# Expert down products all in fp32r, the weight rests made later, and three residual tiles parked in DRAM

## The reference, cut to what matters

```python
def swiglu(h, w_gu, w_down):
    gate, up = jnp.split(h @ w_gu, 2, axis=-1)
    return (jax.nn.silu(gate) * up) @ w_down

def moe_ffn(h, w_router, b_router, w_gu, w_down, w_sh_gu, w_sh_down):
    ...          # scores, top 8 experts of each of the 512 tokens, weights w
    def expert_block(acc, blk):
        tok, wts, e = blk
        out = swiglu(h_pad[tok], w_gu[e], w_down[e])
        return acc.at[tok].add(out * wts[:, None].astype(out.dtype)), None
    ...
    return acc[:N] + swiglu(h, w_sh_gu, w_sh_down)

x_lat = x_lat + gt2 * rms_norm(f_lat.reshape(B, T, D), g_post_ffn[l])
```

## Time and profile before

| | |
|---|---|
| three runs | 2118.14, 2121.33, 2124.74 us; median 2121.33 |
| the profiled execution | 2118.74 us, span of its trace 2117.0 us |
| PE busy | 2042.3 us (96% of the span) |
| DVE / ACT / POOL busy | 1311.6 / 1009.7 / 280.0 us |
| DMA, mean over the span | 186 GB/s; slices of the experts 235 to 385 GB/s |
| TensorE's granted clock | 0.991 of full speed, 1.00 in every stretch of the experts that is quoted below |

### The profile page before, as it was taken

One profiled execution on the slowest core, in us unless ns is written; L12 is line 12 of the kernel. 1 busy time (PEld: TensorE's weight loads), 2 busy tenths in 40 slices (PEclk: granted clock), 3 DMA queues, 4 the chain that ended last, 5 costly groups with the idle time before them and its releaser, 6 DMA issues.

```text
span 2117.0 us, 33346 instructions
## 1 busy us (share of the span) xinstructions
PE 2042.3 (96%) x12264; PEld 1695.0 (80%) x12265; DVE 1311.6 (62%) x1975; ACT 1009.7 (48%) x1475; POOL 280.0 (13%) x217
## 2 busy tenths in 40 slices
PE   8999989999999999999999998999999999999998
PEld 4888977889777667777777768998978898898898
DVE  4878587455788678888868866457642444423433
ACT  4345455223477567777767754334322224312322
POOL 0004032000122332233323310000000000000000
PEclk9999999999999999999999999999999999999999
DMA  9841111263799689999979972211122223222221
GB/s 358 268 145 61 59 45 68 89 253 131 287 346 362 235 302 358 359 361 368 374 264 385 349 278 97 80 61 61 59 81 82 98 83 107 100 80 100 100 80 61
DMA packets 77097, 393.56 MB, mean 186 GB/s; under 512 B 16369, under 2 KB 33009, under 8 KB 46481
## 3 DMA queue, kind: packets, MB, share of 16 engines
q1 hardware_dynamic: 57938, 358.38, 45.1%
q0 software_dynamic: 19008, 33.22, 6.3%
HBM read 384.56 MB, written 43.01 MB: 202 GB/s over the span
## 4 chain that ended last, share of the span: by engine, by line
PE 62%; DMA 5%; DVE 4%; ACT 2%; issue 2%; DVEq 0%; SPq 0%; POOLq 0%; ACTq 0%
PE bank L3449 17%; PE bank L2353 4%; PE bank L2379 4%; PE bank L2357 4%; PE bank L2356 4%; DMA moe_work<-in_experts_dram 3%; PE bank L3132 3%; PE bank L3134 3%; PE bank L3133 3%; PE bank L3117 2%; PE bank L3119 2%; PE bank L3118 2%; PE bank L2339 2%; DVE moe_gu_rest L2114 1%; PE bank L2382 1%
## 5 line engine op out<-in xcount | busy, mean ns | idle before, releaser
L2734 DVE TENSOR_TENSOR b_w_rest<-ring,b_w_high 128x2048 fp32r<-128x2048 f32 x63 | 144.4, 2292 | 180.2 <-ACT b_w_high L2729 179.8
L2353 PE MATMUL bank<-moe_gu_high,moe_x_high 128*128 128x512 f32 x512 | 209.7, 410 | 14.9 <-DVE moe_gu_rest L2114 8.0
L2729 ACT ACTIVATE b_w_high<-ring 128x2048 fp32r<-128x2048 f32 x63 | 120.5, 1913 | 178.4 <-PE bank L3449 126.7
L2357 PE MATMUL bank<-moe_gu_high,moe_x_rest 128*128 128x512 f32 x512 | 201.2, 393 | 0.0
L2356 PE MATMUL bank<-moe_gu_rest,moe_x_high 128*128 128x512 f32 x512 | 201.0, 393 | 0.0
L3133 PE MATMUL bank<-b_w_rest,b_h_high 128*128 128x256 f32 x608 | 171.7, 282 | 0.0
L3132 PE MATMUL bank<-b_w_high,b_h_high 128*128 128x256 f32 x544 | 156.8, 288 | 2.3 <-DVE b_h_rest L2764 1.1
L2114 DVE TENSOR_TENSOR moe_gu_rest<-moe_work,moe_gu_high 128x2048 fp32r<-128x2048 f32 x64 | 146.3, 2288 | 14.4 <-ACT moe_gu_high L1851 14.4
L3134 PE MATMUL bank<-b_w_high,b_h_rest 128*128 128x256 f32 x544 | 154.2, 284 | 0.0
L2114 DVE TENSOR_TENSOR moe_gu_rest<-ring,moe_gu_high 128x2048 fp32r<-128x2048 f32 x64 | 146.5, 2289 | 8.1 <-ACT moe_gu_high L1851 6.9
L3449 PE MATMUL bank<-b_w_high,hidden_high 128*128 128x256 f32 x512 | 144.9, 283 | 0.0
(11 more groups left out here) (525 smaller groups left out, 5340.7 us busy)
## 6 DMA issues: line engine op xcount, KB each, us to landing
ring<-in_stream_dram SPq DMA_DIRECT2D x101, 1024.0 KB, 4.9
moe_work<-in_experts_dram SPq DMA_DIRECT2D x32, 2048.0 KB
moe_work<-in_experts_dram SPq DMA_DIRECT2D x64, 1024.0 KB, 7.3
ring<-in_experts_dram SPq DMA_DIRECT2D x32, 2048.0 KB
X<-in_stream_dram SPq DMA_DIRECT2D x16, 512.0 KB, 9.3
mixer_work<-in_stream_dram SPq DMA_DIRECT2D x16, 512.0 KB, 8.8
mixer_work<-in_stream_dram SPq DMA_DIRECT2D x4, 1024.0 KB, 13.5
X<-in_x_dram SPq DMA_DIRECT2D x8, 512.0 KB, 10.6
```

The source lines that it names most:

```text
L2353: first = mm(banks[2][:, :], xh[:, k, :], wh[h][:, c], start=(k == 0), stop=False)
L2357: last = mm(banks[2][:, :], xl[:, k, :], wh[h][:, c], start=False, stop=(k == KD - 1))
L2734: nc.vector.tensor_tensor(WL[u % FEED], raw(u), high_at(u), ALU.subtract).then_inc(s["w_rest"], 1)
```

## The change

The down product becomes fp32r altogether. For each half k of the contraction there are now a high part DH[p][k] and a rest DL[p][k] of the down weight (two pieces of 128x1024 each on ACT and on DVE, where there was one), and one high part and one rest of the turned hidden rows, 128x256 wide (one piece each, where ACT had two of 128x128 and DVE one). PE issues 12 fp32r products for a block where it issued 2 plain ones (one for each half of the output, 4 records in all) and 6 fp32r ones. The rest of a down weight overwrites its slot.

On DVE dn_rest(u) stands behind w_rest(u+1, 1), and with it behind the further block, of which it stood ahead.

The new buffers lie in X's tiles 1, 2 and 3, so these three are stored to DRAM ahead of the experts (tiles 1 and 2 at the end of the mixer, among the stores of the normalised rows) and loaded back behind them: tile 1 where tile 3 was loaded, tile 3 behind unit 1 of the next block's weights, tile 2 once the last down product is done, ahead of units 2 and 3. Some scratch tiles of the further block move.

The diff, cut to its core (names of scratch tiles, waits that only change their counts in step, are left out):

```diff
@@ -477,8 +477,10 @@
             for t in range(NT):
                 sp.wait_ge(s["h2_ready"], t + 1)
                 sp.dma_start(dram["xn"][t * P:(t + 1) * P, :], H2[:, t, :]).then_inc(s["h2_stored"], 16)
+                if t in (1, 2):
+                    sp.dma_start(dram["parked"][t * P:(t + 1) * P, :], X[:, t, :]).then_inc(s["h2_stored"], 16)
             sp.wait_ge(s["zero_stored"], 32 * NT)
-            sp.wait_ge(s["h2_stored"], 16 * NT)
+            sp.wait_ge(s["h2_stored"], 16 * (NT + 2))
 
         @block.gpsimd
         def _(pool):
@@ -1545,13 +1547,14 @@
     ONEHOT = [grid(mem["place"](f"onehot{k}", EXACT + 816 + 256 * k, 512, BF16)[:, :], 4) for k in range(2)]
     ONEHOTX = grid(mem["place"]("onehot_further", EXACT + 1328, 512, BF16)[:, :], 4)
     CNT = take(NE).bitcast(I32)
-    SG, HID, HDT = take(256), take(256), [take(P) for _ in range(2)]
+    SG, HID = take(256), take(256)
     HDT_AT = at[0]
-    take(256)
-    HDTH = [exact(f"hidden_high{k}", AT_WORK + HDT_AT + P * k, P) for k in range(2)]
-    HDTL = [exact(f"hidden_rest{k}", AT_WORK + WORK + P * k, P) for k in range(2)]
-    DH = [exact(f"down_high{k}", o, D) for k, o in enumerate((AT_X + (NT - 1) * D, EXACT + 1712))]
-    DL = [exact(f"down_rest{k}", AT_WORK + 2 * GU + DN * k + D, D) for k in range(2)]
+    take(512)
+    HDTH = [exact(f"hidden_high{k}", AT_WORK + HDT_AT + 256 * k, 256) for k in range(2)]
+    HDTL = [exact(f"hidden_rest{k}", AT_ADAROW + 512 + 256 * k, 256) for k in range(2)]
+    DH_AT = ((AT_X + D, AT_X + 3 * D), (AT_X + 2 * D, EXACT + 1712))
+    DH = [[exact(f"down_high{p}{k}", DH_AT[p][k], D) for k in range(2)] for p in range(2)]
+    DL = [[exact(f"down_rest{p}{k}", AT_WORK + 2 * GU + DN * p + D * k, D) for k in range(2)] for p in range(2)]
 
     TOKI, ROWI = take(4).bitcast(I32), take(4).bitcast(I32)
     TWA, TWX = take(136).rearrange("p (e c) -> p e c", c=2), [take(2) for _ in range(2)]
@@ -1737,12 +1740,15 @@
             sums_back(1)
             sp.wait_ge(s["dn_done"], NE - 1)
             sp.wait_ge(s["rows_moved"], 32)
-            sp.dma_start(X[:, NT - 1, :], dram["last_rows"][:, :]).then_inc(s["rows_moved"], 16)
+            sp.wait_ge(s["shared_down_in"], 16)
+            sp.dma_start(X[:, 1, :], dram["parked"][P:2 * P, :]).then_inc(s["shared_down_in"], 16)
             unit_in(0)
             sums_back(2)
             sums_back(3)
             unit_in(1)
+            sp.dma_start(X[:, 3, :], dram["parked"][3 * P:4 * P, :]).then_inc(s["rows_moved"], 16)
             sp.wait_ge(s["dn_done"], NE)
+            sp.dma_start(X[:, 2, :], dram["parked"][2 * P:3 * P, :]).then_inc(s["rows_moved"], 16)
             unit_in(2)
             unit_in(3)
             then["sync"](sp)
@@ -1883,15 +1889,16 @@
             def copy_hdt(i, o):
                 after(act, "ht2_done", i, o, 1)
                 after(act, "dn_done", i, o - 2, 1)
-                nc.scalar.activation(HDTH[o % 2], banks[3][:, P:2 * P], ACT.Copy).then_inc(s["down_highs"], 1)
-                nc.scalar.activation(HDT[o % 2], banks[3][:, 0:P], ACT.Copy).then_inc(s["down_highs"], 1)
+                nc.scalar.activation(HDTH[o % 2], banks[3][:, 0:2 * P], ACT.Copy).then_inc(s["down_highs"], 1)
 
             def dn_high(i, o):
                 act.wait_ge(s_dn[o % 2], 16 * (o // 2 + 1) + 32 * i)
                 after(act, "dn_done", i, o - 2, 1)
                 if isinstance(i, int) and 4 * i + o == 0:
                     act.wait_ge(s["rows_moved"], 32)
-                nc.scalar.activation(DH[o % 2], dnslot[o % 2][:, D:2 * D], ACT.Copy).then_inc(s["down_highs"], 1)
+                for k in range(2):
+                    nc.scalar.activation(DH[o % 2][k], dnslot[o % 2][:, D * k:D * (k + 1)], ACT.Copy).then_inc(
+                        s["down_highs"], 1)
 
             def further_split(n):
                 for h in range(2):
@@ -2116,13 +2122,15 @@
 
             def dn_rest(i, o):
 
-                after(dve, "down_highs", i, o, 1, 3)
-                v.tensor_tensor(DL[o % 2], dnslot[o % 2][:, D:2 * D], DH[o % 2], ALU.subtract).then_inc(s["down_rests"], 1)
+                for k in range(2):
+                    after(dve, "down_highs", i, o, 1 + k, 3)
+                    v.tensor_tensor(DL[o % 2][k], dnslot[o % 2][:, D * k:D * (k + 1)], DH[o % 2][k], ALU.subtract).then_inc(
+                        s["down_rests"], 1)
 
             def hdt_rest(i, o):
 
                 after(dve, "down_highs", i, o, 3, 3)
-                v.tensor_tensor(HDTL[o % 2], banks[3][:, P:2 * P], HDTH[o % 2], ALU.subtract).then_inc(s["down_rests"], 1)
+                v.tensor_tensor(HDTL[o % 2], banks[3][:, 0:2 * P], HDTH[o % 2], ALU.subtract).then_inc(s["down_rests"], 1)
 
             def x_rest(i, o):
 
@@ -2169,10 +2177,10 @@
                     x_rest(i, u + 1)
                 if exists(i, u + 3):
                     indices(i, u + 3)
-                dn_rest(i, u)
-                more_blocks(dve, i, u, done, find_further, further)
                 if exists(i, u + 1):
                     w_rest(i, u + 1, 1)
+                more_blocks(dve, i, u, done, find_further, further)
+                dn_rest(i, u)
                 if exists(i, u + 2):
                     block_ahead(dve, i, u + 2, done, find_further)
                 if exists(i, u + 4):
@@ -2276,9 +2285,9 @@
             f_both(3)
             then["w_rest"](dve, 1)
             weighted(2)
+            dve.wait_ge(s["rows_moved"], 64)
             mixed(2)
             weighted(3)
-            dve.wait_ge(s["rows_moved"], 48)
             mixed(3)
             dve.wait_ge(s["f_tile"], 2 * NT)
             for t in (2, 3):
@@ -2360,29 +2369,26 @@
             def turn_hidden(i, o):
                 after(pe, "hid_ready", i, o, 1)
                 after(pe, "down_highs", i, o - 1, 3, 3)
-                after(pe, "down_rests", i, o - 1, 2, 2)
+                after(pe, "down_rests", i, o - 1, 3, 3)
                 for k in range(2):
                     last = nc.tensor.transpose(banks[3][:, k * P:(k + 1) * P], HID[:, k * P:(k + 1) * P], ident)
                 last.then_inc(s["ht2_done"], 1)
 
             def down_ready(i, o, bank=4):
                 after(pe, "down_highs", i, o, 3, 3)
-                after(pe, "down_rests", i, o, 2, 2)
+                after(pe, "down_rests", i, o, 3, 3)
                 if bank == 4:
                     after(pe, "out_act", i, o - 1, 2, 2)
-                pe.wait_ge(s_dn[o % 2], 16 * (o // 2 + 1) + 32 * i)
-
-            def down_products(bank, j, k, o, plain, high, rest):
-
-                c = slice(512 * j, 512 * (j + 1))
-                if k == 0:
-                    return mm(bank[:, :], plain, dnslot[o % 2][:, c], start=True, stop=False)
-                mm(bank[:, :], high, DH[o % 2][:, c], start=False, stop=False)
-                mm(bank[:, :], high, DL[o % 2][:, c], start=False, stop=False)
-                return mm(bank[:, :], rest, DH[o % 2][:, c], start=False, stop=True)
+
+            def down_products(bank, j, k, o, high, rest):
+
+                c, at = slice(512 * j, 512 * (j + 1)), slice(P * k, P * (k + 1))
+                mm(bank[:, :], high[:, at], DH[o % 2][k][:, c], start=(k == 0), stop=False)
+                mm(bank[:, :], high[:, at], DL[o % 2][k][:, c], start=False, stop=False)
+                return mm(bank[:, :], rest[:, at], DH[o % 2][k][:, c], start=False, stop=(k == 1))
 
             def down_part(i, o, j, k, bank=4):
-                product = down_products(banks[bank + j], j, k, o, HDT[o % 2], HDTH[o % 2], HDTL[o % 2])
+                product = down_products(banks[bank + j], j, k, o, HDTH[o % 2], HDTL[o % 2])
                 if (j, k) == (1, 1):
                     product.then_inc(s["dn_done"], 1)
 
@@ -2434,13 +2440,12 @@
                 last.then_inc(s["x_ht"], 1)
 
             def further_down(i, u, n):
-                pe.wait_ge(s["x_he"], 2 * n + 2)
+                pe.wait_ge(s["x_he"], n + 1)
                 pe.wait_ge(s["x_hid"], 2 * n + 2)
-                after(pe, "down_rests", i, u, 1, 2)
-                pe.wait_ge(s_dn[u % 2], 16 * (u // 2 + 1) + 32 * i)
+                after(pe, "down_rests", i, u, 2, 3)
                 for j in range(2):
                     for k in range(2):
-                        last = down_products(banks[6 + j], j, k, u, HDTX, HDTXH, HDTXL)
+                        last = down_products(banks[6 + j], j, k, u, HDTXH, HDTXL)
                     last.then_inc(s["x_dn"], 1)
                 pe.wait_ge(s["x_o"], 2 * n + 2)
 
```

20 lines of the change are left out of this document (10 added, 10 removed).

## The result

The changed kernel takes 2132.5 us (median of 4, 2131.03 to 2136.68); the kernel before, run beside it, 2121.1 us (2118.14 to 2124.74). The ratio is 1.0061, 95% interval 1.0049 to 1.0073: slower by 0.6%, where 0.4% faster (2113 us) was forecast, and outside the range of 2102 to 2127. The profiled execution took 2132.64 us (before: 2118.74), with a span of 2130.9 us.

What follows compares the result with a forecast made beforehand. PE was taken to bound the stage, transfers nearly full. Early experts -7.7, late ones -7.6, further blocks +7.4, start -1.2, end +0.6 summed to -8.5 us: 2121.3 became 2113 us, 8-in-10 range 2102 to 2127.

Steps and rivals of the forecast that it cites:

- Step 6: Further blocks: DVE's new order delays PE's products, +2.6 us a block less 0.2, +7.4 us for three; bounds +4 and +11.
- Step 1: PE's down product: 3.19 us becomes 2.87, saving 0.32 us an expert, so PE could go at 9.65 us.
- Step 2: DVE: a second down rest and a wider hidden rest make 9.75 us an expert; DVE becomes the bound at 9.77.
- DVE's waits stay: Rival, chance 0.13: DVE keeps waits behind PE for hidden(u) and x_rest; at half of them 10.45 us an expert, 2140 us.
- Step 3: ACT: one more high part brings its work from 7.63 to 8.6 us an expert, hidden under 9.77.
- Step 4: Order of rests: gate/up rest no longer behind a late down load, which may come about 2.5 us later before it costs.
- Step 5: Transfers: 376 GB/s taken for a long stretch, so a late expert takes 10.03 us; bounds 10.36 and 9.77.
- transfers at their limit: Rival, chance 0.25: 364 GB/s is all a long stretch gives, late experts stay at 10.36 us; 2126 us at worst.
- The limit of about 358 GB/s: HBM to SBUF transfers: a skill's limit for a core, by which nothing of PE's gain would come out; held for a rival.
- Step 7: Parking residual tiles in DRAM: nothing, at worst 2 us; the last expert's unhidden second down rest +0.6 us.
- only the late experts held by transfers: Case of the transfer rival: late experts gain nothing, early ones reach the forecast pace; 2123 us.
- w = 0.4: DVE's kept wait an expert from which it decides: 30 early experts gain 1.5 us in all, late ones 5, blocks take 7.4.

Runs made afterwards that it cites:

- e2: The kernel before with DVE's new order alone (gate/up rests, further block, then the one down rest), its products unchanged: 2124.2 us.
- e13: The changed kernel without the never-run code for a second and third further block, on PE, ACT and DVE: 2114.2 us.
- e17: The changed kernel with the never-run code for a second and third further block left out of PE's program alone: 2121.6 us.
- e18: The changed kernel with the never-run code for a second and third further block left out of DVE's program alone: 2125.7 us.
- e14: The changed kernel without the never-run code on PE, ACT and DVE, plus useless PE products in three waits of a further block: 2104.2 us.
- e5: The changed kernel with the second gate/up rests and both down rests moved inside the further block, behind its rows' rests: 2125.0 us.
- e10: The changed kernel with those rests inside the further block, but one DVE branch and one count load more per expert instead of two: 2126.6 us.
- e15: The changed kernel without the never-run code, with the rests inside the further block and one DVE branch more per expert: 2112.4 us.
- e1: The changed kernel with DVE's old order back (both down rests ahead of the further block and second gate/up rests): 2166.3 us.
- e8: The changed kernel without further blocks (rows beyond 128 left out), gathers and scatters cut to 16 rows: 2050.4 us.
- e12: The kernel before without further blocks (rows beyond 128 left out), gathers and scatters cut to 16 rows: 2065.6 us.
- e11: The kernel before with the parking alone (tiles 1 and 2 stored, three loads back with their waits): 2121.1 us against 2121.0.
- e9: The changed kernel with useless fp32r products given to PE ahead of three of its waits in a further block: 2273.1 us.

## Why the prediction was wrong

**Step 6, the further block, is the step that failed.** +7.4 us was the forecast, +11 its far end. The nine intervals 12 to 16 and 45 to 48 took 25.0 us more (4.0 + 11.9 + 9.2), though the ordinary ones among them should have gained 1 to 2. Two delays that the step named were there: 2.50 us of PE's idle time before the further down product, 7.5 in all, and DVE's gate/up rest ahead of the rows' rests. What its sum lacked is three terms:

- The search for the block, for which PE waited 5.4 us instead of 0.6. The step had it, a us for each, in its far end alone; the waits were 1.4, 1.6 and 2.4 us.
- A wait of 4.8 us for the gathered rows of the third block, which no step had. e2 has 7.4 us of such waits, e13, e17 and e18 have none, so it does not come every time, and what decides that is not settled.
- The clock. Behind some of these waits a few microseconds ran at half clock. By the rows that is at most (1 - 0.78) x 15.45 + 0.09 x 78.26 + 0.08 x 63.37 = 15.5 us, at most because it counts PE's idle time at half clock as lost too. e14 recovered 8.0 in two stages by keeping PE busy.

The windows of before for intervals 13 to 16 and 45 to 48 show how this adds up:

```profile
701.25:767.64 66.39, 61.96 (x286) 44.59 (x285) 38.86 (x61) 37.07 (x54) 18.89 (x11) 1.00 0.65 219
1051.80:1105.98 54.18, 51.18 (x242) 37.45 (x241) 36.87 (x57) 33.76 (x47) 17.77 (x10) 1.00 0.79 277
```

PE was idle for 4.4 + 3.0 us in them and is idle for 12.5 + 11.0 us in after: 16.1 of the 21.1 us more are waits. The other 5.0 are PE's busy time, which grew although its products take less: that is the clock.

The rests could also have stood in DVE's idle time of 5.78 us, which I read and set against nothing; there they take off 15 to 17 us (e5, e10).

**Step 1** was right: 2.86 us, products 0.23 us apart, intervals of 9.6 us.

**Step 2** mis-sized DVE. It is busy 151.89 / 16 = 9.49 us an expert, not 9.75, and hardly waits, so PE and DVE are nearly level at 9.5 to 9.6, and the rival "DVE's waits stay" is out. How little room DVE has shows when a branch is added (e10, e15: 0.3 us or more in three of four intervals).

**Step 3**: ACT is busy 132.72 / 16 = 8.3 us, hidden. Right.

**Step 4** was right and worth more than I gave it: with the old order the products cost 34 us more (e1). The chain of the earlier trace rows is gone, the wait of the earlier trace rows too.

**Step 5**, 376 GB/s in a long stretch: 371 in after, 383 in e18. Intervals 33 to 44 and 49 to 60 gained 6.7 us, near the 6.9 that 10.03 us an expert gives; that is luck in part, for the first twelve gained 0.8 and the last twelve 5.8. The rival "transfers at their limit" had the mechanism (e8, e12) but overstated it. The limit of about 358 GB/s that I weighed there does not bind here: 383 ran for 117 us. The Trainium skill (DMA: Bandwidth & Descriptors, section Bandwidth) gives it as the share of each core when both cores of a pair stream; with one core at work, as here, its own figure is the 425, and 383 is under that. So my sentence that by the page nothing would come out read it too narrowly.

**What no step had**: the first eleven intervals, +3.9 us (111.06 to 114.96) where 11 x 9.77 gives -3.6. e17 shows that it is PE's program: the three waits among the first eight experts. In the profile of before they were one wait of 1.2 us for nothing, at 619.77, which I let stand as one stall (2.6 us at the same place in e2, whose program on PE is the same). Why they grew to 7.1 us, when 9 packets came over q8 in both, is not settled; that a faster PE comes to its program sooner is a guess that no run tests.

**Step 7** was right: e11 is at 0.9984 to 1.0012, and the part behind the last load did not move.

Two sums among the rivals were wrong. With only the late experts held by transfers, -7.7 + 7.4 - 0.6 is -0.9, so 2120 us and not 2123. And at w = 0.4 the early experts take 10.15 us against 10.13, so they gain nothing, and not 1.5 us.

Of the 22 us between the sum of -8.5 and the 13.9 that came, the blocks with interval 12 explain some 19 and the first eleven intervals 7.5; the start, intervals 17 to 32 and 49 to 60 and the end were better than forecast and give the rest back.

## What to carry to other kernels

Where an engine waits in a rare block, count every wait, that of a search or gather ahead of the block too, and what PE's clock does behind it: here the blocks' two stages took 8.0 us less once PE was kept busy (e13, e14). Before rests or copies are moved behind a block, look for an idle stretch inside it. And count the code: the code of a branch that is never taken cost 18 us of 2132 here, and 192 more products in a loop's code some 150.

## What the hardware showed that was not expected

- PE's clock fell to half behind, or late in, 7 of the 12 waits of 1.4 us or more that PE had among the experts of after, and stayed full at the other five, among them two of 2.5 and 2.6 us. The same wait of 1.60 us ahead of the first further block was followed by half clock in after and by full clock in e13 and e17. Among the experts of before no wait was above 1.3 us, and the clock stayed full. Work of no use in those waits kept it full but for some 3 us (e14 against e13). So a wait does not by its length alone tell what the clock will do.
- PE's loop of four experts ran without fetching in after (no packets on q8 in 540 us) and in e14, with 96 products more and the code never run left out; with 192 more and all code in (e9) it was fetched in each pass, with stalls of up to 9.6 us between 800 and 1040 us that the trace shows as waits for nothing.
- Transfers at a DMA share of 1.0 carried 371 or 383 GB/s, with the length of DVE's program the only difference between the two kernels (after, e18). Why is open.
